# A two-layer transformer block with experts: the smallest expert class holds 32 tokens instead of 64

## The chip, the core and the metric

The kernel runs on one core of one Trainium2 chip. Its time is the time of one execution on the device in microseconds (us). A program is written once for each engine: PE (TensorE, the matrix engine; PEld is its loading of weights), DVE (VectorE), ACT (ScalarE) and SP (SyncE, which here only issues DMA transfers). Engines and transfers meet through semaphores.

## What is computed

Two layers over 256 tokens of width 1024. Each layer has a token mixer (four kinds of attention, four heads each) and a feed-forward part, both between an adaptive norm and a residual. The feed-forward part of layer 0 is dense. That of layer 1 is a mixture of eight experts, of which each token uses the two with the largest router logits:

```python
def _swiglu(h, wg, wu, wd):
    return (jax.nn.silu(h @ wg) * (h @ wu)) @ wd

logits = h.astype(jnp.float32) @ w_router.astype(jnp.float32)     # 8 experts
top_val, top_idx = lax.top_k(logits, TOP_K_EXPERTS)               # 2 of 8
gate = jax.nn.softmax(top_val, axis=-1)
...
return _swiglu(xb, w_gate[e], w_up[e], w_down[e])                 # 1024 -> 3584 -> 1024
...
y_assign = ys[dest] * g_s[:, None].astype(h.dtype)
return jnp.zeros_like(h).at[tok_s].add(y_assign)
```

All is float32. With the inputs of `setup_inputs()` the reference sends 25, 54, 96, 70, 145, 10, 84 and 28 tokens to experts 0 to 7.

## The kernel before

**Everything ahead of the experts** (layer 0 whole, layer 1 up to the router) is one straight program for each engine and is not touched by the change, but for the line numbers. It ends at 749 us of the profiled execution.

**The experts** run one after the other in a hardware loop over `r` (L967, eight rounds). Each expert's 3584 hidden channels are cut into four steps (`ES`), so there are 32 steps `J`. A step needs 896 gate columns, 896 up columns (1024 rows each) and 896 down rows (1024 columns). SP loads them with a program of its own (L521 to L538) in a fixed order: four pieces of gate weights, four of up weights (896 KB each), two pieces of down weights (1536 KB) and a last one in two halves (256 KB each), 10,752 KB or 11.01 MB a step. **The buffer holds one step.** A piece of step J+1 is issued only when PE has used the same piece of step J for the last time (`g_used`, `u_used`, `d_used`), and SP issues strictly in order.

**Classes.** DVE sorts each expert by its number of tokens against `CAPS` into class 1 to 4, and each engine branches on it (L971, L1371, L1565). The code of all four classes stands in the loop, one after the other. `UNITS` says how the tokens of a class are laid out on PE's columns: "half" is 64 tokens, so that two groups of 448 hidden channels are worked on side by side; "quarter" is 32 tokens, four groups side by side (gate low, gate high, up low, up high, all in bank 2); "wide" is 128 tokens and one group. Class 1 is one half, class 2 a half and a quarter, class 3 a wide and a quarter. By the counts above, experts 0, 1, 5 and 7 are class 1, experts 2, 3 and 6 class 2, expert 4 class 3, and class 4 isn't used.

**A step of class 1 on PE**: `hidden` for gate and for up (32 products, L829), each waiting for its own weight pieces as they land; ACT's SiLU and DVE's product with the up half (L1342); `turn_hidden` transposes the result (L854, L859); ACT copies it (L1522); `down` multiplies with the down rows (14 products, L879). Class 2 does the same, then `quarter` (L841, 32 products) between `hidden` and `turn_hidden`, and a second, smaller transposition and `down` (28 products) at the end. In class 2 and 3 the last user of gate and up weights is `quarter`, so `g_used` and `u_used` are signalled there.

**At the end of an expert** ACT (L1557) and DVE (L1350 to L1361) copy the outputs out of PSUM, PE scatters them to the tokens (`scatter`, L954 and L962), DVE adds them up (L1380), clears the banks, and the loop turns to the next expert. DVE makes the next expert's window of tokens (`window`, L1312) while PE is still in the last step.

Of the kernel before, what the change touches and what calls it, by code (L numbers as in the profile page):

```python
# [30 lines left out]
ACT = mybir.ActivationFunctionType  # L31
AX_X = mybir.AxisListType.X

P = 128
T = 256
D = 1024
KC = D // P
# [15 lines left out]
ES = 4  # L53
# [166 lines left out]
def ada_after(l, at):  # L220
# [3 lines left out]
    while i < len(STREAM) and STREAM[i][0] == "ada":  # L224
# [7 lines left out]

CAPS = (64, 96, 160)
UNITS = {1: [("half", 0)], 2: [("half", 0), ("quarter", 64)], 3: [("wide", 0), ("quarter", 128)],
         4: [("wide", 0), ("wide", 128)]}
ITEMS = {n: sum(2 if kind == "wide" else 1 for kind, _ in units) for n, units in UNITS.items()}

# [33 lines left out]
def build(nc, x, c, w_ada, b_ada, g_mix, w_in, g_heads, w_out, g_ffn, w_ff_gate, w_ff_up, w_ff_down,  # L273
          w_router, w_exp_gate, w_exp_up, w_exp_down, g_final, ctab_in, btab_in, out):
    with ExitStack() as ctx:
# [59 lines left out]
        ys = part(2 * D).rearrange("p (q n) -> p q n", q=2)  # L335
# [32 lines left out]
        hs = moe[:, 2 * EH:4 * EH].rearrange("p (b n) -> p b n", b=2)  # L368
# [7 lines left out]
        bank = [ctx.enter_context(nc.psum_tensor(f"bank{i}", [P, CW], F32)) for i in range(8)]  # L376
# [25 lines left out]
        full_u = [sem(f"up_in{i}") for i in range(KP)]  # L402
# [39 lines left out]
        def done(n, i):  # L442

            return i + 1 if i < ITEMS[n] - 1 else 4
# [104 lines left out]
        def _(pe):  # L549
# [284 lines left out]
                    elif (n == 1 and k == KC - 2) or (not last_item and k == KC - 1):  # L834
                        last.then_inc((eg_p, eu_p)[a], 3 if n == 1 else before_last(n, i))

            def quarter(t0, ks):

                for k in ks:
                    for q, w in enumerate((eg, eg, eu, eu)):  # L840
                        last = mm(bank[2][32 * q:32 * q + 32, 0:EH], xsT[:, k, t0:t0 + 32],  # L841
                                  w[:, k, (q % 2) * EH:(q % 2 + 1) * EH], start=(k == 0), stop=(k == KC - 1))
                        if k % 2 and q % 2:
                            last.then_inc(u_used if q == 3 else g_used, 1)

            def turn_hidden(J, n, i, kind, o, c=0):

                if kind != "quarter":
                    pe.wait_ge(eh_v, 4 * J + done(n, i))
                rows_ = slice(64, P) if kind == "quarter" else slice(0, P)  # L850
                h, one_ = hs[rows_, i % 2, :], ident[rows_, rows_]
                m = 64 if kind == "quarter" else P
                for t in range(3):
                    nc.tensor.transpose(o[:, t * m:(t + 1) * m], h[:, t * P:(t + 1) * P], one_)  # L854
                if kind == "wide":
                    last = mm(o[64 * c:64 * c + 64, 3 * P:4 * P], h[:, 3 * P:EH], ident, start=True, stop=True)
                else:
                    for c2 in range(2):
                        last = mm(o[64 * c2:64 * c2 + 64, 3 * m:3 * m + m // 2], h[:, 3 * P:EH],  # L859
                                  one_[:, c2 * m // 2:(c2 + 1) * m // 2], start=True, stop=True)  # L860
                last.then_inc(et_p, share(n, i))
# [25 lines left out]
            def step(r, J, n):  # L887
# [1 line left out]
                A = UNITS[n][0]  # L889
                B = UNITS[n][1] if len(UNITS[n]) > 1 else None  # L890
                if n == 1:
                    hidden(J, n, 0, 0, A)
                    hidden(J, n, 0, 1, A)
                    turn_hidden(J, n, 0, "half", bank[3])
                    pe.wait_ge(yzero_v, r + 1)
                    down(J, n, 0, ALL, (0,))
                elif n == 2:
                    hidden(J, n, 0, 0, A)
# [79 lines left out]
        def _(ve):  # L978
# [4 lines left out]
            def signal(ins, s):  # L983

                ins.then_inc(s, 1)
                count[s.name] = count.get(s.name, 0) + 1
# [358 lines left out]
            def expert_end(r, n):  # L1345

                window(r + 1)
                tiles = 2 if n > 2 else 1
                ve.wait_ge(sgt_p, r + 1)
                last = nc.vector.tensor_copy(selgT[:, 0:tiles, :].rearrange("p q n -> p (q n)"), bank[0][:, 0:tiles * T])  # L1350
                if n > 1:
                    ve.wait_ge(d_used, 3 * ES * r + 3 * ES)
                if n in (2, 3):
                    s0, q = (64, 0) if n == 2 else (0, 1)
                    for c in range(4):
                        last = nc.vector.tensor_copy(ys[s0:s0 + 32, q, c * T:(c + 1) * T],
                                                     bank[6][32 * c:32 * c + 32, 0:T])
                elif n == 4:
                    for hf in range(2):
                        last = nc.vector.tensor_copy(ys[:, 1, hf * CW:(hf + 1) * CW], bank[6 + hf][:, :])  # L1360
                last.then_inc(ys_v, 1)  # L1361
# [2 lines left out]
            clear_banks()  # L1364
            scatter_weights(0)
            signal(nc.vector.memset(ys, 0.0), dv)
            signal(nc.vector.memset(yacc, 0.0), yacc_v)
            with ve.Fori(0, NE) as r:
                which = class_of(ve, r)
# [28 lines left out]
        def _(ae):  # L1398
# [126 lines left out]
            def step(J, n):  # L1525

                if n == 1:
                    silu(J, n, 0)
                    turned_hidden(J, n, 0, 0, 0, bank[3])
                elif n == 2:  # L1530
                    silu(J, n, 0)
                    turned_hidden(J, n, 0, 0, 0, bank[3])
# [19 lines left out]
            def expert_end(r, n):  # L1552

                ae.wait_ge(d_used, 3 * ES * r + 3 * ES)
                for hf in range(2):
                    if UNITS[n][0][0] == "half":
                        ins = act(ys[0:64, 0, hf * CW:(hf + 1) * CW], bank[4][64 * hf:64 * hf + 64, :], ACT.Copy)  # L1557
                    else:
                        ins = act(ys[:, 0, hf * CW:(hf + 1) * CW], bank[4 + hf][:, :], ACT.Copy)
                ins.then_inc(ys_a, 1)  # L1560
# [26 lines left out]
```

## Time and profile before

| | us |
|---|---|
| median of 3 runs | 1781.99 |
| lowest, highest | 1771.41, 1783.42 |
| the profiled execution: its own time | 1774.51 |
| its span, from the first to the last instruction | 1772.7 |
| start of expert 0 to start of expert 1 | 749.6 to 850.6 |
| expert 1 | 850.6 to 973.1 |
| expert 2 | 973.1 to 1098.1 |
| expert 3 | 1098.1 to 1221.4 |
| expert 4 | 1221.4 to 1426.4 |
| last product of expert 7 ends | 1758.3 |

Each expert's start is the start of its first product on PE; expert 1's is taken as the end of the scatter before it, at 850.59, since PE stands idle behind that (the rows show it). PE is busy for 90% of the span, and DMA for 74% of it. The chain of waits follows the work that ended last back through the trace: each of its rows is a start time, a length and what was under way. A row "PE bank L830 x64" is 64 records, two for each of 32 products, since each float32 product appears as two matrix records and two weight loads.

### The profile page before, as it was taken

The page shows a single profiled execution, that of the slowest core. Times are in us where ns is not written, and L with a number is a line of the kernel's source. Part 1 is how long each engine was busy: PE and PEld are TensorE (multiplying, and loading weights), DVE is VectorE, ACT ScalarE, POOL GpSimd, SP SyncE. Part 2 cuts the span into 40 slices and gives each one's busy share as a digit, 9 for nine tenths or more (in the row PEclk, how much of TensorE's full clock was granted, in tenths as well). Part 3 has the DMA queues.
Part 4 walks back from the last instruction along what each step waited for, and adds up shares of the span by engine and source line. Part 5 has one row for each costly group of instructions (what it writes and reads, how often), then busy time and mean ns, then how long its engine had stood idle before and what let it go on. Part 6 is the DMA issues. An engine that isn't in the chain of part 4 may idle for free.

```text
span 1772.7 us, 19682 instructions
## 1 busy us (share of the span) xinstructions
PE 1594.6 (90%) x8282; PEld 872.2 (49%) x8283; DVE 409.1 (23%) x867; ACT 226.2 (13%) x439; POOL 0.2 (0%) x4
## 2 busy tenths in 40 slices
PE   5999889999989998797597999999999998999975
PEld 5778658777658784432132333334444433333321
DVE  4265523323333633400101002002000110100103
ACT  1122210000011321110011011111011001111101
POOL 0000000000000000000000000000000000000000
PEclk9999899999989998799799999999999999999998
DMA  9955525665745440099999999897666599999995
GB/s 348 326 203 177 190 95 190 237 237 190 262 136 181 167 181 19 3 378 371 342 389 371 382 378 370 327 389 279 248 248 235 208 327 388 370 389 371 389 371 217
DMA packets 168108, 482.18 MB, mean 272 GB/s; under 512 B 10472, under 2 KB 20992, under 8 KB 167936
## 3 DMA queue, kind: packets, MB, share of 16 engines
q1 hardware_dynamic: 168064, 481.57, 74.3%
q8 instruction: 30, 0.49, 0.1%
q14 instruction: 14, 0.11, 0.0%
HBM read 480.49 MB, written 1.05 MB: 272 GB/s over the span
## 4 chain that ended last, share of the span: by engine, by line
PE 74%; SPq 8%; DVE 8%; DMA 6%; issue 3%; ACT 2%; DVEq 0%; ACTq 0%
PE bank L830 14%; PE bank L879 10%; PE bank L640 7%; SPq L527 6%; PE bank L841 6%; PE bank L777 6%; PE bank L826 6%; PE bank L791 4%; DMA ring<-in_w_exp_down 4%; DVE acc L1004 4%; PE bank L759 3%; PE bank L873 3%; PE bank L634 2%; PE bank L962 2%; SPq L533 1%
## 5 line engine op out<-in xcount | busy, mean ns | idle before, releaser
L830 PE MATMUL bank<-ring,hT 128*64 128x448 f32 x1792 | 353.8, 545 | 45.6 <-issue 19.3
L879 PE MATMUL bank<-ring,bt 128*32 128x256 f32 (+1 forms) x1680 | 239.9, 495 | 24.5 <-DMA ring<-in_w_exp_down 12.3
L830 PEld LDWEIGHTS bank<-ring,hT 128*64 128x64 f32 x1792 | 130.0, 137 | 265.9 <-issue 205.9
L1342 DVE TENSOR_TENSOR bt<-bt,bank 128x448 f32<-128x448 f32 (+1 forms) x52 | 32.4, 622 | 807.6 <-PE bank L830 555.0
L879 PEld LDWEIGHTS bank<-ring,bt 128*32 128x32 f32 (+1 forms) x1680 | 86.0, 125 | 160.5 <-issue 119.1
L777 PE MATMUL bank<-hT,ring 128*128 128x256 f32 x704 | 156.0, 383 | 1.2 <-DVE hT L1075 1.2
L640 PE MATMUL bank<-hT,ring 128*128 128x256 f32 x640 | 152.9, 396 | 2.3 <-ACT hT L1424 1.2
L777 PEld LDWEIGHTS bank<-hT,ring 128*128 128x128 f32 x704 | 134.6, 192 | 21.7 <-issue 1.9
L640 PEld LDWEIGHTS bank<-hT,ring 128*128 128x128 f32 x640 | 124.4, 198 | 23.4 <-DVE hT L1075 3.1
L1004 DVE SCALAR_TENSOR_TENSOR acc<-ring,cond,acc 128x512 f32<-128x512 f32 x160 | 120.3, 752 | 5.6
L841 PE MATMUL bank<-ring,hT 128*32 128x448 f32 x1024 | 102.9, 542 | 0.0
L826 PE MATMUL bank<-ring,hT 128*128 128x448 f32 x256 | 98.2, 542 | 0.0
L791 PE MATMUL bank<-ring,arena 128*128 128x512 f32 x176 | 76.7, 594 | 0.0
L1510 ACT ACT_TABLE_LOAD x32 | 41.1, 1283 | 249.5 <-PE bank L830 246.6
L826 PEld LDWEIGHTS bank<-ring,hT 128*128 128x128 f32 x256 | 48.1, 190 | 47.0 <-issue 47.0
L1522 ACT ACTIVATE bt<-bank 128x448 f32<-128x448 f32 (+1 forms) x44 | 21.0, 476 | 331.1 <-PE bank L859 331.1
L759 PE MATMUL bank<-ring,hT 128*128 128x512 f32 x128 | 59.2, 625 | 2.0 <-DVE hT L1072 2.0
L634 PE MATMUL bank<-ring,hT 128*128 128x256 f32 x256 | 57.1, 381 | 3.1 <-ACT arena L1444 3.1
L841 PEld LDWEIGHTS bank<-ring,hT 128*32 128x32 f32 x1024 | 30.0, 109 | 59.8 <-issue 58.9
L634 PEld LDWEIGHTS bank<-ring,hT 128*128 128x128 f32 x256 | 48.1, 190 | 10.8 <-issue 4.5
L791 PEld LDWEIGHTS bank<-ring,arena 128*128 128x128 f32 x176 | 33.1, 190 | 39.7 <-issue 39.7
L873 PE MATMUL bank<-ring,bt 128*128 128x512 f32 x112 | 50.2, 600 | 0.0
(204 smaller groups left out, 999.8 us busy)
## 6 DMA issues: line engine op xcount, KB each, us to landing
ring<-in_w_exp_gate SPq DMA_DIRECT2D x128, 896.0 KB, 10.4
ring<-in_w_exp_up SPq DMA_DIRECT2D x128, 896.0 KB, 15.1
ring<-in_w_exp_down SPq DMA_DIRECT2D x64, 1536.0 KB, 16.3
ring<-in_w_ada SPq DMA_DIRECT2D x24, 2048.0 KB, 10.4
ring<-in_w_in SPq DMA_DIRECT2D x10, 2048.0 KB, 11.1
ring<-in_w_exp_down SPq DMA_DIRECT2D x64, 256.0 KB, 16.8
ring<-in_w_ff_gate SPq DMA_DIRECT2D x5, 2048.0 KB, 18.6
ring<-in_w_ff_up SPq DMA_DIRECT2D x5, 2048.0 KB, 14.0
```

The costliest lines, as they stand in the source:

```text
L527: sp.dma_start(dst[:, 2 * i:2 * i + 2, :], w[0, e, 2 * i * P:2 * (i + 1) * P, j0:j0 + EW].rearrange("(c p) n -> p c n", p=P))\
L634: last = mm(o[:, b * T:(b + 1) * T], hT[:, k, b * P:(b + 1) * P], w[:, k, :], start=(k == 0), stop=(k == KC - 1))
L640: last = mm(o[:, 0:T], w[:, k, t * P:(t + 1) * P], hT[:, k, :], start=(k == 0), stop=(k == KC - 1))
L759: last = mm(bank[4 + 2 * hf + b][:, :], hT[:, k, b * P:(b + 1) * P], w[:, k, :], start=(k == 0), stop=(k == KC - 1))
L777: last = mm(bank[n % 2][:, a * T:(a + 1) * T], w[a][:, k, t * P:(t + 1) * P], hT[:, k, :], start=(k == 0), stop=(k == KC - 1))
L791: last = mm(bank[4 + 2 * hf + b][:, :], ffT[:, (j - 1) % 2, r, b * P:(b + 1) * P], w[:, r, hf * CW:(hf + 1) * CW], start=(j == 1 and r == ...
L826: last = mm(o[:, 0:EH], xsT[:, k, t0:t0 + P], w[:, k, c * EH:(c + 1) * EH], start=(k == 0), stop=(k == KC - 1))
L830: last = mm(o[64 * c2:64 * c2 + 64, 0:EH], xsT[:, k, t0:t0 + 64], w[:, k, c2 * EH:(c2 + 1) * EH], start=(k == 0), stop=(k == KC - 1))
L841: last = mm(bank[2][32 * q:32 * q + 32, 0:EH], xsT[:, k, t0:t0 + 32], w[:, k, (q % 2) * EH:(q % 2 + 1) * EH], start=(k == 0), stop=(k == K ...
L873: last = mm(bank[4 + 2 * u + hf][:, :], hsT[:, u, t * P:(t + 1) * P], ed[:, t, hf * CW:(hf + 1) * CW], start=False, stop=True, skip_group_ ...
L879: last = mm(bank[4 + 2 * u][m * c:m * c + m, 0:D // parts], hsT[:, u, at_:at_ + m], ed[:, t, c * (D // parts):(c + 1) * (D // parts)], sta ...
L1004: ins = stt(acc[:, :], w[:, k, :], cond[:, k:k + 1], acc[:, :], ALU.mult, ALU.add)
```

## The change

`CAPS` starts at 32, and class 1 is one unit "quarter" instead of one "half". An expert with 33 to 64 tokens is now class 2. With the counts above experts 0, 5 and 7 stay in class 1, which has a new body, and expert 1 (54 tokens) moves to class 2; the others keep both class and body.

In class 1 PE now works gate and up side by side, `k` by `k`, and waits for a gate piece and the up piece with the same number together. It signals `g_used` and `u_used` from the same loop. `down` has 28 products of 256 columns instead of 14 of 512. The transposition handles half as many columns, except for one transposition of the full height. The output copies cover 32 instead of 64 tokens and are shared by ACT and DVE; DVE waits for `d_used` there. DVE clears `hs` once, ahead of the loop.

```diff
--- before.py
+++ after.py
@@ -232,8 +232,8 @@
 
 
 
-CAPS = (64, 96, 160)
-UNITS = {1: [("half", 0)], 2: [("half", 0), ("quarter", 64)], 3: [("wide", 0), ("quarter", 128)],
+CAPS = (32, 96, 160)
+UNITS = {1: [("quarter", 0)], 2: [("half", 0), ("quarter", 64)], 3: [("wide", 0), ("quarter", 128)],
          4: [("wide", 0), ("wide", 128)]}
 ITEMS = {n: sum(2 if kind == "wide" else 1 for kind, _ in units) for n, units in UNITS.items()}
 
@@ -834,23 +834,32 @@
                     elif (n == 1 and k == KC - 2) or (not last_item and k == KC - 1):
                         last.then_inc((eg_p, eu_p)[a], 3 if n == 1 else before_last(n, i))
 
-            def quarter(t0, ks):
+            def quarter(t0, ks, J=None):
 
                 for k in ks:
+                    if J is not None and k % 2 == 0:
+                        pe.wait_ge(full_g[k // 2], 16 * J + 16)
+                        pe.wait_ge(full_u[k // 2], 16 * J + 16)
                     for q, w in enumerate((eg, eg, eu, eu)):
                         last = mm(bank[2][32 * q:32 * q + 32, 0:EH], xsT[:, k, t0:t0 + 32],
                                   w[:, k, (q % 2) * EH:(q % 2 + 1) * EH], start=(k == 0), stop=(k == KC - 1))
                         if k % 2 and q % 2:
                             last.then_inc(u_used if q == 3 else g_used, 1)
+                        elif J is not None and k == KC - 1:
+                            last.then_inc(eu_p if q == 2 else eg_p, 3)
 
             def turn_hidden(J, n, i, kind, o, c=0):
 
                 if kind != "quarter":
                     pe.wait_ge(eh_v, 4 * J + done(n, i))
+                if n == 1:
+                    pe.wait_ge(eh_v, 4 * J + done(n, i))
+                    nc.tensor.transpose(o[:, 0:P], hs[:, 0, 0:P], ident)
+                    o = o[:, 64:]
                 rows_ = slice(64, P) if kind == "quarter" else slice(0, P)
                 h, one_ = hs[rows_, i % 2, :], ident[rows_, rows_]
                 m = 64 if kind == "quarter" else P
-                for t in range(3):
+                for t in range(1 if n == 1 else 0, 3):
                     nc.tensor.transpose(o[:, t * m:(t + 1) * m], h[:, t * P:(t + 1) * P], one_)
                 if kind == "wide":
                     last = mm(o[64 * c:64 * c + 64, 3 * P:4 * P], h[:, 3 * P:EH], ident, start=True, stop=True)
@@ -889,10 +898,9 @@
                 A = UNITS[n][0]
                 B = UNITS[n][1] if len(UNITS[n]) > 1 else None
                 if n == 1:
-                    hidden(J, n, 0, 0, A)
-                    hidden(J, n, 0, 1, A)
-                    turn_hidden(J, n, 0, "half", bank[3])
+                    quarter(A[1], range(KC), J)
                     pe.wait_ge(yzero_v, r + 1)
+                    turn_hidden(J, n, 0, "quarter", bank[3])
                     down(J, n, 0, ALL, (0,))
                 elif n == 2:
                     hidden(J, n, 0, 0, A)
@@ -1348,13 +1356,13 @@
                 tiles = 2 if n > 2 else 1
                 ve.wait_ge(sgt_p, r + 1)
                 last = nc.vector.tensor_copy(selgT[:, 0:tiles, :].rearrange("p q n -> p (q n)"), bank[0][:, 0:tiles * T])
-                if n > 1:
-                    ve.wait_ge(d_used, 3 * ES * r + 3 * ES)
-                if n in (2, 3):
-                    s0, q = (64, 0) if n == 2 else (0, 1)
-                    for c in range(4):
+                ve.wait_ge(d_used, 3 * ES * r + 3 * ES)
+                if n < 4:
+                    s0, q = ((0, 0), (64, 0), (0, 1))[n - 1]
+                    o = bank[4 if n == 1 else 6]
+                    for c in ((2, 3) if n == 1 else range(4)):
                         last = nc.vector.tensor_copy(ys[s0:s0 + 32, q, c * T:(c + 1) * T],
-                                                     bank[6][32 * c:32 * c + 32, 0:T])
+                                                     o[32 * c:32 * c + 32, 0:T])
                 elif n == 4:
                     for hf in range(2):
                         last = nc.vector.tensor_copy(ys[:, 1, hf * CW:(hf + 1) * CW], bank[6 + hf][:, :])
@@ -1364,6 +1372,8 @@
             clear_banks()
             scatter_weights(0)
             signal(nc.vector.memset(ys, 0.0), dv)
+            signal(nc.vector.memset(hs, 0.0), dv)
+            own(dv)
             signal(nc.vector.memset(yacc, 0.0), yacc_v)
             with ve.Fori(0, NE) as r:
                 which = class_of(ve, r)
@@ -1526,7 +1536,7 @@
 
                 if n == 1:
                     silu(J, n, 0)
-                    turned_hidden(J, n, 0, 0, 0, bank[3])
+                    turned_hidden(J, n, 0, 0, 0, bank[3][:, 64:])
                 elif n == 2:
                     silu(J, n, 0)
                     turned_hidden(J, n, 0, 0, 0, bank[3])
@@ -1553,7 +1563,9 @@
 
                 ae.wait_ge(d_used, 3 * ES * r + 3 * ES)
                 for hf in range(2):
-                    if UNITS[n][0][0] == "half":
+                    if n == 1:
+                        ins = act(ys[0:32, 0, hf * T:(hf + 1) * T], bank[4][32 * hf:32 * hf + 32, 0:T], ACT.Copy)
+                    elif n == 2:
                         ins = act(ys[0:64, 0, hf * CW:(hf + 1) * CW], bank[4][64 * hf:64 * hf + 64, :], ACT.Copy)
                     else:
                         ins = act(ys[:, 0, hf * CW:(hf + 1) * CW], bank[4 + hf][:, :], ACT.Copy)
```

How the order moves. The first place is class 1 on PE, inside the loop over experts (`ring` holds the weights, `hT` the expert's tokens, `bt` the hidden values, `arena` the outputs and scatter matrices). Before:

```order
L972 ISA
L830 MATMUL bank<-ring,hT 64x448 x32
L849 ISA
L854 MATMUL bank<-ct,bt 128x128 x3
L859 MATMUL bank<-ct,bt 64x64 x2
L879 MATMUL bank<-ring,bt 64x512 x12
L870 ISA
L879 MATMUL bank<-ring,bt 64x512 x2
L972 REGISTER_ALU
L972 COMPARE_AND_BRANCH
```

Of the change:

```order
L844 MATMUL bank<-ring,hT 32x448 x32
L856 ISA
L857 MATMUL bank<-ct,bt 128x128
L863 MATMUL bank<-ct,bt 128x64 x2
L868 MATMUL bank<-ct,bt 64x32 x2
L888 MATMUL bank<-ring,bt 32x256 x24
L879 ISA
L888 MATMUL bank<-ring,bt 32x256 x4
```

The first phase has as many products as before, each for 32 instead of 64 tokens; the down phase has twice as many, each of half the width. The class-1 code on PE is longer by 14 products.

The second place is class 1 on DVE with the end of the expert (the row `bt<-bt,bank` is the product of SiLU and up half, `hT<-ring` the next expert's window, `arena<-bank` the copies out of PSUM). Before:

```order
L1342 TENSOR_TENSOR bt<-bt,bank 128x448
L1372 REGISTER_ALU
L1372 COMPARE_AND_BRANCH
L1311 ISA
L1311 TENSOR_LOAD route_i
L1311 ISA x2
L1312 ISA
L1312 COPY hT<-ring 128x2048
L1350 COPY arena<-bank 128x256
```

Of the change:

```order
L1350 TENSOR_TENSOR bt<-bt,bank 64x448
L1382 REGISTER_ALU
L1382 COMPARE_AND_BRANCH
L1319 ISA
L1319 TENSOR_LOAD route_i
L1319 ISA x2
L1320 ISA
L1320 COPY hT<-ring 128x2048
L1358 COPY arena<-bank 128x256
L1359 ISA
L1364 COPY arena<-bank 32x256 x2
```

Two small copies and a wait have come behind the copy of the scatter matrix; the rest stands as it did.

## Rows read from the trace of the kernel before

**Rows 1.** The page: chain that ended last, shares by engine

```profile
PE 74%; SPq 8%; DVE 8%; DMA 6%; issue 3%; ACT 2%; DVEq 0%; ACTq 0%
```

**Rows 2.** Chain of waits, experts 0 and 1: start us, length us, what

```profile
749.62 12.27 PE bank L830 x64
...
764.24 6.23 PE bank L879 x28
...
841.86 3.70 PE bank L879 x16
846.92 3.67 PE bank L962 x8
850.59 19.28 issue
869.87 14.62 PE bank L830 x64
...
962.72 5.38 PE bank L879 x16
...
973.13 12.18 PE bank L830 x64
```

**Rows 3.** Chain of waits, class 2: experts 2 and 3, start of 4

```profile
985.31 4.65 PE bank L841 x48
...
1002.37 12.18 PE bank L830 x64
...
1085.06 5.03 PE bank L879 x64
...
1098.11 12.18 PE bank L830 x64
...
1210.04 5.03 PE bank L879 x64
...
1221.39 18.04 PE bank L826 x48
```

**Rows 4.** Chain of waits, experts 5 to 7

```profile
1426.38 12.20 PE bank L830 x64
...
1537.10 1.72 PE bank L830 x8
...
1749.58 3.68 PE bank L879 x16
```

**Rows 5.** Stretches: length, busy PE, PEld, DVE, ACT, POOL, clock, DMA share, GB/s

```profile
850.60:869.90 19.30, 0.03 (x2) 0.03 (x2) 3.13 (x7) 0.00 (x0) 0.00 (x0) 0.59 1.01 367
869.90:874.00 4.10, 4.10 (x12) 1.48 (x14) 0.00 (x0) 0.00 (x0) 0.00 (x0) 0.50 0.34 121
...
1432.00:1752.00 320.00, 286.15 (x1684) 104.96 (x1682) 26.57 (x45) 34.41 (x48) 0.00 (x0) 0.97 1.03 377
```

**Rows 6.** Timeline of SP's DMA issues: start us, length us, line, target, count

```profile
751.38 4.88 SPq L527 DMA_DIRECT2D ring<-in_w_exp_gate  x4
...
873.16 5.70 SPq L527 DMA_DIRECT2D ring<-in_w_exp_gate  x4
...
1111.96 5.76 SPq L527 DMA_DIRECT2D ring<-in_w_exp_gate  x4
```

**Rows 7.** DMA queue q8, packets, MB, share: whole span, 0:733, 848:872

```profile
q8 instruction: 30, 0.49, 0.1%
...
q8 instruction: 24, 0.39, 0.2%
...
q8 instruction: 6, 0.10, 2.6%
```

**Rows 8.** Groups by line and shape, experts only: busy us, mean ns | idle before

```profile
L830 PE MATMUL bank<-ring,hT 128*64 128x448 f32 x1792 | 353.8, 545 | 45.6 <-issue 19.3 <-DMA ring<-in_w_exp_up 12.7 <-DMA ring<-in_w_exp_gate 10.8
...
L841 PE MATMUL bank<-ring,hT 128*32 128x448 f32 x1024 | 102.9, 542 | 0.0
...
L879 PE MATMUL bank<-ring,bt 128*32 128x256 f32 x896 | 51.7, 381 | 0.0
```

## The prediction

> **What bounds the kernel now.** I read the chain of waits first. By shares it is a PE kernel [rows 1], but the share is a mean over stages, so I followed the chain through the experts in order of time, and then asked in each stage whether PE or the weight stream is late.
>
> *Class 1 is late on DMA.* Expert 0 starts at 749.62 with its first step's weights in place: 12.27 us of hidden products, then 6.23 us of down products [rows 2]. A step of pure PE work, with what lies between, is thus under 21 us. The last down weights of its fourth step let PE go on only at 841.86 [rows 2], 92 us after the start. The stream moves 377 GB/s when nothing stops it [rows 5]; 11.01 MB a step at that rate are 29.2 us. Three steps of it from the first issue at 751.38 [rows 6] end at 839, which is where PE waits.
>
> *Class 2 is late on PE, by a hair.* A step of class 2 lasts from 973.13 to 1002.37, 29.24 us, all of it PE, with `quarter` starting at 985.31 [rows 2, 3]. To an undisturbed stream this is the same as 29.2. The difference between the classes is not in the step, but in **when the first weight piece is given back**. In class 1 that is 751.38, 1.8 us after the expert's start [rows 2, 6]. In class 2 gate piece 0 is free only in `quarter`: expert 3 starts at 1098.11, and the stream restarts at 1111.96, 13.85 us later [rows 3, 6].
>
> *The PE gap at 850.59.* Behind expert 0's scatter PE waits 19.28 us for nothing that a semaphore shows [rows 2], and its clock falls to 0.59 [rows 5]. The weights of expert 1's first step stream in meanwhile at 367 GB/s, and by 869.9 they are nearly done: in the next 4.1 us the DMA share is 0.34 [rows 5]. The next step's issue follows at 873.16 [rows 6], so the stream stands for only some 2 us. What PE waits for is its own code: of 30 packets on the instruction queue q8, 24 come ahead of 733 us, six in 848 to 872, and so none later [rows 7]. The first round skips the code of classes 2 to 4 and jumps back; that code is fetched through the full DMA queues, six packets in about three round trips of 6.4 us. It happens once.
>
> **The Trainium skill on this wait.** "Runtime: NRT & Kernel Launch", section "Instruction fetch mechanics", says that an engine's code is streamed in 16 KiB blocks, that a jump out of what is held waits for a fetch, and that PE holds 128 KiB, 2048 instructions. The six packets of 0.10 MB agree with the block size. By my count of the built program the loop over experts is some 1,710 PE instructions before and 1,770 after, so by the page's figure it still fits and this wait stays a single one; what would follow if it didn't is a rival below.
>
> **The change, part by part.** Weights, SP's order and the work of experts 2, 3, 4 and 6 are the same.
>
> *Class 1's hidden products get cheaper where it isn't wanted.* A record of `quarter` costs 102.9/1024 = 100 ns against 353.8/1792 = 197 ns for `hidden` [rows 8]: 64 records are 6.4 instead of 12.3 us. Down: 56 records at 51.7/896 = 58 ns are 3.2 instead of 6.2 us [rows 2, 8]. That is 9 us less PE in each of 12 steps, 108 us in sum, all of it under the stream, which takes 29.2 us a step whatever PE does. The new wait pairs gate piece 0 with up piece 0, which lands four pieces (9.4 us of stream) later, and what queues behind it on PE is only the other products; by then six pieces, 7.2 MB or 19 us of stream, are still issued, so the release is not late and SP does not run dry. At the start of an expert both pieces are there and piece 0 is free after 16 records of 100 ns, 1.6 us, as now. The stream of expert 0 and of experts 5 to 7 therefore keeps its times. For 5 to 7 the check is that eleven steps (121 MB at 377 GB/s, 321 us) from 1428 (expert 5's start at 1426.38 plus 1.6) end at 1749, and PE's last weights came at 1749.58 [rows 4]. Sum of this part: 0. The later SiLU (it now needs all of the gate, behind the last piece) is covered too: down weights land 9 us behind the last up piece. Without that cover it would cost under 2 us.
>
> *Tails.* What is left behind the last weights gets shorter at experts 0 and 7: one down tile (0.9 to 0.45 us) and smaller output copies. I take -0.8 us each. Against it stands the clock: PE now idles in one piece while four gate pieces and the first up piece land (4.6 MB, 12 us of each step), and after the idle stretch at 850.59 the first 64 records took 14.62 instead of 12.2 us [rows 2, 3]; the last down products may run as at 962.72, 5.38 instead of 3.70 us for the same 16 records [rows 2]. With a slow scatter this is up to +3.5 us. I take -0.8 for expert 0 and 0 for expert 7.
>
> *Expert 1 moves to class 2.* This is the term that decides. It starts where PE comes out of the gap: 850.59 - 0.8 + 19.3 = 869.1. The code of class 1 is 56 PE instructions longer (14 products, four instructions each), which shifts what lies in which block: between nothing and one more round trip of 6.4 us, of which the last would be short, as the weights are in by then. I take +2: 871.1. Its hidden products run cold for 14.6 us, `quarter` starts at 885.7 and gives piece 0 back 1.7 us later, at 887.4. The stream has run dry at about 872. **It now stands for 15 us instead of 2.** From there PE sets the pace: 2.5 us of cold start, four steps of 29.24 us, and the expert's end. From the start of the last 64 down records to the next expert it took 13.05 us at 1085.06 and 11.35 at 1210.04 [rows 3], so 8.0 and 6.3 behind the records; I take 7.2. Expert 1 ends at 871.1 + 2.5 + 117.0 + 7.2 = 997.8 instead of 973.1: **+24.7 us**. Nothing gives this back: expert 2 before started with a full stream too and took 125.0 us, PE-bound; as a successor of class 2 it should take what expert 3 took, 123.3 to 125.0: -0.8. Experts 3 and 4 are PE-bound and move whole. Experts 5 to 7 are a chain of stream hung on expert 5's start, so they move whole too.
>
> *DVE's clearing of `hs`* ahead of the loop (under 1.8 us) lies beside the first hidden products: 0.
>
> Sum: 24.7 - 0.8 = **+23.9 us**, the rest 0. On the profiled execution, 1774.5, that is 1798.4; its time is 7.5 under the median, and on the median the sum would give 1805.9. I forecast **1800 us**, nearer the profiled one, since the sum was made on it.
>
> **Rivals.**
>
> *The stream does not break (not slower).* If PE's code is there sooner, expert 1 starts sooner. The new piece 0 has to be free before 872, so the start has to lie before 872 - 12.2 - 1.7 = 858, that is the gap has to be shorter than about 8 us instead of 19.3. For it: the longer class 1 reaches further into its neighbour's code, which could be fetched in the quiet of the first steps. Against: three of the four classes' blocks are still ahead of the jump. Then hidden products wait for the stream, expert 1 ends at about 977, and the time is +4 us: 1779 to 1786.
>
> *The loop's code no longer stays in.* If the 56 instructions push it over what PE holds, the gap of 850.59 comes at every change of expert. At four PE-bound changes that is 4 times 19.3 us on top, +77, and some of it at the others: 1875 to 1900. For it: the loop grew by a few per cent, and the trace shows only that the old size fits. By the page's figure it fits still.
>
> *The clock.* If class 1 idles enough for half clock all through, its step is 2 times 9.6 us and some 4 of waits, 23 us, still under 29.2; only the tails grow. +27 to +30 us: 1801 to 1812.
>
> *Faster.* Experts 0, 5 and 7 have 108 us less PE work; this would only show if the stream were not what they wait for, against rows 4 and 5.
>
> **How the numbers follow.** Forecast as worked out (+17 to +27) 0.61, stream unbroken 0.15, code pushed out 0.08, clock low in class 1 0.12, faster or other 0.04. The range leaves out the pushed-out code and the lower half of the unbroken stream: 1785 to 1813. A measurement tells about 1% from no change (17.8 us). The forecast is 1.3%, so about a tenth of its chance falls under that with the unbroken stream: same 0.22; slower 0.75; faster 0.03.
>
> **What would show it.** In the changed kernel: an idle stretch of PE behind expert 0 of 19 to 26 us with six or seven packets on q8; the next gate issue 15 to 18 us behind expert 1's first product; a DMA share near 0 between; steps of 29.2 us in expert 1, and expert 2 starting near 998; experts 5 to 7 as long as before, 332 us from 5's start to 7's last product. I am wrong if q8 moves after the first round, if the gate issue comes early, or if class 1's steps shorten.

## The result

The changed kernel takes 1799.18 us, the median of 4 runs (1792.11 to 1802.74), against 1776.70 us for the kernel before (4 runs of the same session, 1769.66 to 1783.42). The ratio is **1.0138 (95% interval 1.0088 to 1.0188)**: 22.5 us slower, where the forecast was 1800 us and a sum of +23.9 us. Run twice more later, each time beside before, it came out at 1.0168 (1.0118 to 1.0218; I had expected 1.010 to 1.015 of that run) and 1.0112 (1.0070 to 1.0154).

The execution profiled took 1802.74 us, its span 1800.8 us. Its chain of waits, in the stretches that rows 2 show of before (start us, length us, what; L844 is `quarter`, L888 `down`, L970 `scatter`):

```profile
751.64 6.23 PE bank L844 x62
...
845.07 3.17 PE bank L888 x32
...
850.25 3.70 PE bank L970 x8
853.95 17.82 issue
871.77 14.59 PE bank L830 x64
...
903.42 12.18 PE bank L830 x64
...
997.46 12.18 PE bank L830 x64
...
1120.74 12.18 PE bank L830 x64
...
1245.72 18.04 PE bank L826 x48
...
1450.95 6.19 PE bank L844 x62
...
1562.39 1.72 PE bank L830 x8
...
1775.37 3.64 PE bank L888 x32
...
1781.01 5.42 PE bank L970 x8
```

Expert 0 starts 2.0 us later than before (nothing ahead of it was changed) and takes 102.3 us where before took 101.0 [rows 2]. The gap behind it is 17.8 instead of 19.3 us. Then expert 1, now class 2, takes 125.7 us to expert 2's start, where before took 103.3. Experts 2 and 3 take 123.3 and 125.0 us (before 125.0 and 123.3 [rows 3]), expert 4 205.2 (205.0), and experts 5 to 7 up to the end of the last scatter 335.5 (331.9).

SP's timeline, for rows 6:

```profile
753.37 4.88 SPq L527 DMA_DIRECT2D ring<-in_w_exp_gate  x4
...
888.03 5.76 SPq L527 DMA_DIRECT2D ring<-in_w_exp_gate  x4
```

and the stretches of expert 0, the gap, the break in the stream, the rest of expert 1, and experts 5 to 7 (length, then busy PE, PEld, DVE, ACT and POOL, granted clock, DMA share, GB/s):

```profile
753.00:850.00 97.00, 55.26 (x498) 19.96 (x490) 9.86 (x14) 9.45 (x14) 0.00 (x0) 0.75 1.01 364
853.00:871.00 18.00, 0.95 (x3) 0.12 (x1) 3.82 (x8) 0.00 (x0) 0.00 (x0) 0.58 1.03 389
...
874.00:888.00 14.00, 14.00 (x80) 5.10 (x80) 0.62 (x1) 0.54 (x1) 0.00 (x0) 0.91 0.04 13
888.00:997.00 109.00, 106.75 (x834) 40.02 (x826) 9.43 (x16) 13.70 (x21) 0.00 (x0) 1.00 1.01 371
1460.00:1775.00 315.00, 231.35 (x1844) 85.10 (x1843) 26.80 (x46) 30.59 (x46) 0.00 (x0) 0.84 1.03 380
```

In class 1 PE is busy for 55 of 97 us and the stream goes on at 364 GB/s; in the last row PE has 55 us less work than rows 5 show for a stretch of about the same length, and the stream is as full as before (1.03). After expert 1's start the stream stands for 14 us (share 0.04), until `quarter` gives the first piece back 16.3 us after the start. The groups of the experts say the same by line (busy us, mean ns, idle before):

```profile
L844 PE MATMUL bank<-ring,hT 128*32 128x448 f32 x2048 | 221.1, 576 | 77.2 <-DMA ring<-in_w_exp_up 74.4
...
L830 PE MATMUL bank<-ring,hT 128*64 128x448 f32 x1024 | 198.7, 546 | 18.9 <-issue 17.8
```

What PE no longer works in class 1 it waits for up pieces instead: 74.4 us ahead of L844.

### The profile page after: what moved, and what is told of

Same layout as the page of the kernel before. It is cut to its first block, busy times and chain, and to the rows that moved or that the text cites. A ratio compares the mean times of both kernels' runs of the same rounds, so it can differ in the third digit from the quotient of the medians.

```text
span 1800.8 us, 21465 instructions
## 1 busy us (share of the span) xinstructions
PE 1559.8 (87%) x9126; PEld 862.0 (48%) x9127; DVE 416.6 (23%) x882; ACT 226.1 (13%) x447; POOL 0.2 (0%) x4
## 4 chain that ended last, share of the span: by engine, by line
PE 74%; DMA 11%; DVE 7%; SPq 4%; issue 2%; ACT 1%; DVEq 0%
PE bank L830 10%; PE bank L844 10%; PE bank L888 9%; DMA ring<-in_w_exp_up 8%; PE bank L640 7%; PE bank L777 6%; PE bank L826 5%; PE bank L791 4%; DVE acc L1012 4%; PE bank L759 3%; SPq L527 3%; PE bank L882 3%; DMA ring<-in_w_exp_down 2%; PE bank L634 2%; PE bank L970 2%
## 5 line engine op out<-in xcount | busy, mean ns | idle before, releaser
L844 PE MATMUL bank<-ring,hT 128*32 128x448 f32 x2048 | 221.1, 576 | 77.2 <-DMA ring<-in_w_exp_up 74.4
L888 PE MATMUL bank<-ring,bt 128*32 128x256 f32 (+1 forms) x2240 | 232.6, 477 | 15.8 <-DMA ring<-in_w_exp_down 9.6
L1350 DVE TENSOR_TENSOR bt<-bt,bank 64x448 f32<-64x448 f32 (+1 forms) x56 | 34.9, 623 | 834.9 <-ACT bt L1518 388.5
L830 PE MATMUL bank<-ring,hT 128*64 128x448 f32 x1024 | 198.7, 546 | 18.9 <-issue 17.8
L844 PEld LDWEIGHTS bank<-ring,hT 128*32 128x32 f32 x2048 | 66.0, 115 | 214.0 <-issue 212.7
L888 PEld LDWEIGHTS bank<-ring,bt 128*32 128x32 f32 (+1 forms) x2240 | 89.5, 127 | 144.5 <-issue 93.4
L830 PEld LDWEIGHTS bank<-ring,hT 128*64 128x64 f32 x1024 | 72.6, 138 | 140.7 <-issue 136.9
L640 PEld LDWEIGHTS bank<-hT,ring 128*128 128x128 f32 x640 | 126.1, 201 | 23.9 <-DVE hT L1083 3.1
L1532 ACT ACTIVATE bt<-bank 128x224 f32<-128x224 f32 (+1 forms) x48 | 20.1, 420 | 304.6 <-PE bank L868 304.6
L970 PE MATMUL bank<-arena 128*128 128x512 f32 x72 | 39.8, 707 | 15.6 <-DVE arena L1364 15.6
L634 PEld LDWEIGHTS bank<-ring,hT 128*128 128x128 f32 x256 | 48.1, 190 | 10.8 <-issue 4.5
```

The source lines that it names most:

```text
L634: last = mm(o[:, b * T:(b + 1) * T], hT[:, k, b * P:(b + 1) * P], w[:, k, :], start=(k == 0), stop=(k == KC - 1))
L640: last = mm(o[:, 0:T], w[:, k, t * P:(t + 1) * P], hT[:, k, :], start=(k == 0), stop=(k == KC - 1))
L830: last = mm(o[64 * c2:64 * c2 + 64, 0:EH], xsT[:, k, t0:t0 + 64], w[:, k, c2 * EH:(c2 + 1) * EH], start=(k == 0), stop=(k == KC - 1))
L888: last = mm(bank[4 + 2 * u][m * c:m * c + m, 0:D // parts], hsT[:, u, at_:at_ + m], ed[:, t, c * (D // parts):(c + 1) * (D // parts)], sta ...
L970: last = mm(bank[4 + 2 * b + hf][:, :], selgT[:, q, b * P:(b + 1) * P], ys[:, q, hf * CW:(hf + 1) * CW], start=(q == 0), stop=(q == tiles[ ...
```

## The experiments

Theory: expert 1's move to class 2 is the whole loss. In class 1 PE has 8 us a step to spare against the stream and makes up for the gap behind expert 0; in class 2 it has none, so the gap and 29.2 us a step add up. Rivals: the new class-1 body costs something itself; the break in the stream, not PE's pace, makes expert 1 long; the gap is something else than code.

The kernels' stages, read off their traces as above (us; "0" and the rest are experts up to the start of the next one's first product or, for 0 and 7, to the end of the scatter; one execution each; each ratio is to before in its own session, where before's median was 1775.6 to 1776.7):

| kernel | median, ratio to before | 0 | gap | 1 | 2 to 4 | 5 to 7 |
|---|---|---|---|---|---|---|
| before | 1776.7 | 101.0 | 19.3 | 103.3 | 453.3 | 331.9 |
| changed | 1799.2, 1.0138 | 102.3 | 17.8 | 125.7 | 453.5 | 335.5 |
| changed, second | 1804.0, 1.0168 | 103.0 | 18.0 | 125.3 | 453.5 | 331.0 |
| changed, third | 1797.5, 1.0112 | 105.6 | 14.9 | 125.7 | 453.5 | 335.1 |
| cap 32, old body | 1799.3, 1.0129 | 98.6 | 19.5 | 125.1 | 453.5 | 339.0 |
| quarter and half | 1780.8, 1.0022 | 105.1 | 15.6 | 102.2 | 456.2 | 338.8 |
| changed, no class-4 code | 1803.1, 1.0154 | 101.3 | 12.2 | 125.6 | 453.5 | 339.0 |
| the same, again | 1801.6, 1.0108 | 103.6 | 12.0 | 126.3 | 451.7 | 344.8 |
| changed, class-1 code last | 1780.0, 1.0031 | 102.2 | none | 128.8 | 453.5 | 332.5 |
| before, class-1 code last | 1779.3, 1.0012 | 102.4 | none | 119.7 | 455.0 | 335.2 |
| changed, fewer down rows | 1768.6, 0.9988 | 93.3 | 18.3 | 126.5 | 451.8 | 312.5 |
| five classes, no class-4 code | 1781.2, 1.0020 | 103.2 | 18.4 | 98.9 | 452.6 | 338.5 |

The column "5 to 7" follows the weight stream. With all weights loaded it runs from 331.0 to 344.8 us, the changed kernel alone from 331.0 to 335.5. The four executions without class-4 code on PE ("quarter and half" is one of them) are all at 338.5 or more, and six of the seven with it at 335.5 or less; "cap 32, old body", at 339.0, breaks the pattern. No run looks for a cause, so this column can hide a few us of any edit.

The gap and expert 0 have to be read together. In the changed kernel's three traces PE's first product of expert 1 starts 17.9, 18.0 and 17.9 us after the first code packet behind expert 0 (packets at 853.9, 851.4 and 848.5 us). In the third the gap is only 14.9 us because the scatter before it ran at the lower clock, most of its records in 1.06 instead of 0.59 us, while the fetch was already under way:

```profile
844.94 6.55 PE bank L970 x8
851.49 14.91 issue
```

So its 3 us more in expert 0 are 3 us less in the gap. The same holds for "quarter and half".

**The class without the body.** The kernel before, with one line changed:

```diff
-CAPS = (64, 96, 160)
+CAPS = (32, 96, 160)
```

> The kernel before with CAPS (32, 96, 160) and nothing else: experts 0, 5 and 7 keep the old half body, expert 1 is class 2. Theory (the loss is expert 1's move, the cheaper body of class 1 lies under the weight stream): as slow as the changed kernel or 1 to 4 us less, since its tails are not cold, so 20 us above before, ratio about 1.011; expert 1 takes about 143 us with the gap, expert 5 to the end as before. Rival 1 (the lighter body is worth something): clearly slower than the changed kernel, up to 108 us. Rival 2 (the new body costs, by its paired waits or by the clock): within 5 us of before.

Chain of waits of this kernel behind expert 0:

```profile
845.00 19.51 issue
864.51 13.99 PE bank L830 x64
...
989.61 12.18 PE bank L830 x64
```

Measured: 1799.29 us, ratio 1.0129 (1.0094 to 1.0164). It is the changed kernel's time, with PE's old 20 us of work a step in class 1. Expert 1 takes 125.1 us behind the gap. So the cheaper body is worth nothing in time, in either direction that these runs can tell, and the whole loss comes with expert 1's class.

**The body without the class.** The changed kernel with the old half body for 33 to 64 tokens, in the place of class 4:

```diff
-         4: [("wide", 0), ("wide", 128)]}
+         4: [("half", 0)]}
...
+                elif n == 4:
+                    hidden(J, n, 0, 0, A)
+                    hidden(J, n, 0, 1, A)
+                    turn_hidden(J, n, 0, "half", bank[3])
+                    pe.wait_ge(yzero_v, r + 1)
+                    down(J, n, 0, ALL, (0,))
...
-            then(ts(total, sums, float(CAPS[0]), 1.0, ALU.is_gt, ALU.add))
-            for cap in CAPS[1:]:
+            then(ts(total, sums, float(CAPS[0]), -1.0, ALU.is_gt, ALU.add))
+            for _ in range(2):
+                then(stt(total, sums, float(CAPS[0]), total, ALU.is_gt, ALU.add))
+                then(stt(total, sums, 64.0, total, ALU.is_le, ALU.add))
+            for cap in CAPS[1:2]:
```

> The changed kernel with one more class: up to 32 tokens the new quarter body, 33 to 64 the old half body, which stands in the place of the unused class of 160 to 256 tokens. Expert 1 is on the half body again. Theory: all of the loss goes but the longer tails of experts 0 and 7: 0 to 4 us above before. Rival 2 (the new body costs by itself): 10 us or more above before. If the cheap body were a gain, it would be under before.

Measured: 1780.80 us, ratio 1.0022 (0.9996 to 1.0048). Expert 1 is back at 102.2 us behind the gap. Both halves of the change are now priced: the class some 23 us (by the run before, 17 to 29), the body 4 us (its interval is -0.7 to +8.5). So the body is worth nothing within some us; closer than that these runs don't tell.

**A shorter jump.** Class 4's code, which no expert of these inputs runs, is left out of PE's loop:

```diff
-                for n in range(1, 5):
+                for n in range(1, 4):
                     with pe.If(which == n):
```

> The changed kernel without the code of the unused fourth class on TensorE (467 instructions less to jump over; no expert of these inputs is in it). Theory (PE waits behind expert 0 for its own code, and expert 1 in class 2 can't catch up): four packets behind expert 0 on the instruction queue instead of five, the gap 11 to 13 us instead of 17.8, and the time 5 to 7 us under the changed kernel. Rival (the gap is a wait for weights or semaphores): gap and time unchanged.

Chain of waits of this kernel behind expert 0, and its instruction queue in 845 to 866 us; then the queue of the changed kernel in 853 to 874 us:

```profile
847.73 3.70 PE bank L970 x8
851.43 12.23 issue
...
q8 instruction: 4, 0.07, 1.8%
```

```profile
q8 instruction: 5, 0.08, 2.1%
```

One packet and 5.6 us less: the gap behaves as a wait for code. But the time, 1803.05 us, ratio 1.0154 (1.0118 to 1.0190), is not lower, against my expectation. In the trace the saving reaches expert 5's start (692.6 us after expert 0's, against 699.3), and half of it is gone by the last scatter, 3.2 us less than in the changed kernel's first trace. So I ran it again beside the changed kernel.

> The changed kernel without the fourth class's code on TensorE, a second time, now in one call with the changed kernel itself, since the first time its trace showed the gap 5.6 us and expert 1 as much shorter and the total did not. Theory: gap 12 us, expert 1 137 to 138 us, median 3 to 7 us under the changed kernel of this call. Rival (the 6 us are given back in the stages that follow the stream): experts 5 to 7 together 5 us longer than in the changed kernel, in this execution too, and the medians equal.

> The changed kernel, the yardstick of this call. Theory: 1.3 to 1.7% above before; gap 17 to 20 us, experts 2 to 4 within 2 us of the earlier traces, expert 5's start to the last product of expert 7 between 331 and 339 us, as in the executions seen so far.

Measured: 1801.59 us, ratio 1.0108 (1.0068 to 1.0148), and 1797.45 us, 1.0112 (1.0070 to 1.0154) for the changed kernel. The gaps are 12.0 and 14.9 us (12.1 and 17.9 from the first code packet). The changed kernel is under the 1.3% and its gap under the 17 us that I had expected of it; the gap is explained above. The totals are equal within what six runs tell. Up to expert 5's start the kernel without class-4 code is again 6 us shorter (693.6 against 699.7), and again its stream stage is longer (344.8 against 335.1), as the rival said. Whether that is the scatter of single executions or a way in which the gain is given back, these runs do not settle.

**No jump under load.** Class 1's code is placed last on PE, so that expert 0 already has to get past the others, when the DMA queues are idle; the wait for the expert's tokens goes into the step:

```diff
+                pe.wait_ge(xsT_v, r + 1)
                 A = UNITS[n][0]
...
-                pe.wait_ge(xsT_v, r + 1)
-                for n in range(1, 5):
+                for n in (2, 3, 4, 1):
                     with pe.If(which == n):
```

> The changed kernel with the code of class 1 placed last in TensorE's loop (classes 2, 3, 4, 1), so that expert 0 already has to jump over the others, while the DMA queues are idle. Theory: the code packets come around 747 to 758 us, the gap of 17.8 us behind expert 0 goes, expert 0 starts 3 to 8 us later; the next gate issue after expert 0 comes near or before the end of the stream; the time is 8 to 15 us under the changed kernel, but still 5 to 12 above before. Rival (the gap belongs to the turn of the loop, not to the fetched code): gap and time stay.

Chain of waits of this kernel, SP's timeline behind expert 0, and the instruction queue in 735 to 752 us (in 760 to 1775 us it has no packet):

```profile
744.24 2.86 issue
747.11 7.93 PE bank L844 x62
...
861.00 1.72 PE bank L830 x8
...
890.89 1.72 PE bank L830 x8
...
951.22 1.73 PE bank L830 x8
...
977.96 12.17 PE bank L830 x63
```

```profile
864.39 5.76 SPq L527 DMA_DIRECT2D ring<-in_w_exp_gate  x4
```

```profile
q8 instruction: 6, 0.10, 2.7%
```

Measured: 1780.02 us, ratio 1.0031 (1.0003 to 1.0059), 17 to 24 us under the changed kernel's three medians, more than the 8 to 15 expected. The later start of expert 0 that I had expected isn't there: the first packet comes at 736.3 us, while PE is still in its last product ahead of the experts, which ends at 742.1. From that packet to the first product it takes 10.8 us, of which only 2.9 are a wait of their own; behind expert 0 it takes 17.9, nearly all of it waiting. Expert 1, still class 2, now ends every hidden phase on the arrival of an up piece (the short L830 rows at 861.0, 890.9 and 951.2): PE has caught up with the stream. This is the rival "the stream does not break", made true; I had priced it at 977 us for expert 1's end, and it ended at 977.96.

**The gap alone.** The same edit on the kernel before.

> The kernel before with TensorE's code of class 1 placed last in the loop, as in the earlier experiment on the changed kernel. Theory (with expert 1 in class 1 the gap is made up for by PE's spare 8 us a step, and only the 2 us for which the stream stood are to be had, against 3 us of later start): within 5 us of before, no gap behind expert 0. Rival (the gap costs before its full 19 us too): 10 to 15 us under before.

Measured: 1779.30 us, ratio 1.0012 (0.9981 to 1.0043). Its chain of waits:

```profile
744.49 3.03 issue
747.51 13.90 PE bank L830 x64
...
969.49 12.18 PE bank L830 x64
```

The whole 19.3 us gap is gone from the chain and the time is the same, since expert 1 in class 1 then waits for the stream: 119.7 us, where gap and body took 122.5. A wait that the next stage can catch up on is worth nothing.

The four kernels together, from expert 0's start to expert 5's: class 1 with the gap (before) 676.8 us, without it 677.0; class 2 with the gap (changed) 699.3, without it 684.3. So the gap alone costs nothing, class 2 alone 7 to 8 us, and both together 22.5: two thirds of the loss is there only when both are. These are single executions; by the ratios it is +2 us, +6 and +20 to +30.

**A lighter stream.** The changed kernel loads two of three row tiles of each large down piece; the products over the third run on what the buffer held:

```diff
-                    sp.dma_start(ed[:, 3 * i:3 * i + 3, :],
-                                 w_exp_down[0, e, r0:r0 + 3 * P, :].rearrange("(c p) n -> p c n", p=P)).then_inc(full_d[i], 16)
+                    sp.dma_start(ed[:, 3 * i:3 * i + 2, :],
+                                 w_exp_down[0, e, r0:r0 + 2 * P, :].rearrange("(c p) n -> p c n", p=P)).then_inc(full_d[i], 16)
```

> The changed kernel with a third of the down rows of each large down piece not loaded (two tiles of three; the products over the third run on what the buffer held before), so a step streams 9.96 instead of 11.01 MB, and all of PE's work is left. Theory (class 1 follows the stream, class 2 and 3 follow PE): expert 0 about 8 us shorter, expert 1 behind the gap (about 126 us) and experts 2, 3 and 4 unchanged, expert 5 about 8 to 11 us shorter, expert 7 8 to 15 us shorter: 25 to 35 us under the changed kernel. Rival (expert 1 is long since its stream starts late): expert 1 behind the gap is 8 us shorter too. Rival (class 1 is bound by something on PE): its stages keep their length.

Its chain of waits around expert 1, and its stretch from 888 to 980 us:

```profile
838.83 3.70 PE bank L970 x8
842.53 18.33 issue
...
981.92 5.40 PE bank L970 x8
```

```profile
888.00:980.00 92.00, 91.66 (x738) 34.61 (x736) 5.26 (x8) 9.47 (x17) 0.00 (x0) 1.00 0.94 345
```

Measured: 1768.59 us, 29 to 35 us under the changed kernel's medians. Expert 0 is 9 us shorter or more and experts 5 to 7 are 18 to 23 us shorter, of which 6 to 7 in expert 5, where I had expected 8 to 11. **Expert 1 keeps its length (126.5 us)**, with PE busy for 91.7 of 92 us. The break in the stream is still there (a share of 0.01 from 861 to 876 us, where the next piece is issued); but each step now has 2.8 us less to stream behind it, and expert 1 gains nothing by that. So it is not the late stream that makes expert 1 long.

**More code.** The old half body as a fifth class, so that nothing is dropped. By my count of the compiled program PE's loop has 1998 instructions, against 1706 before and 1766 of the changed kernel.

```diff
-         4: [("wide", 0), ("wide", 128)]}
+         4: [("wide", 0), ("wide", 128)], 5: [("half", 0)]}
...
-                for n in range(1, 5):
+                for n in range(1, 6):
```

> The changed kernel with the old half body as a fifth class behind the fourth (33 to 64 tokens), so that all old classes stay. TensorE's loop has 1998 instructions instead of 1766. Theory (the loop's code is fetched once, as long as it stays under the 2048 instructions that the Trainium skill's page Runtime: NRT & Kernel Launch gives): one or two more packets on the instruction queue behind expert 0 and none later, time 1779 to 1787. Rival (code is pushed out of what TensorE holds): packets and a gap of 10 to 25 us at every change of expert, 60 to 110 us above before.

The page's row for its instruction queue, and its chain of waits at each change of expert:

```profile
q8 instruction: 92, 1.51, 0.4%
```

```profile
853.79 35.92 issue
...
990.33 8.90 issue
...
1125.83 18.78 issue
...
1270.20 25.21 issue
...
1502.76 7.22 issue
...
1615.50 28.97 issue
...
1771.01 17.48 issue
```

Measured: 1910.14 us, ratio 1.0751 (1.0681 to 1.0821), 134 us above before. There are 92 packets instead of 30 and a gap at each of the seven changes of expert, 142 us in all. My theory was wrong here: I took the figure of the Trainium skill, "Runtime: NRT & Kernel Launch", section "Instruction fetch mechanics" (2048 instructions for PE), as the bound. By the trace 1998 already do not stay in, and the measurement decides. Why the bound lies lower, no run shows. So I left class 4 out of PE's loop of this same kernel:

```diff
-                for n in range(1, 6):
+                for n in (1, 2, 3, 5):
```

> The kernel with five classes, of which TensorE's loop leaves out the code of the unused fourth: 1531 instead of 1998 instructions, all else as in the five-class kernel. Theory (its 134 us were code that no longer stays in): packets only ahead of expert 0 and behind it, none later, 1776 to 1784 us, as with the four classes quarter, half, 96 and 160. Rival (the fifth class costs by its numbering, or by what the other engines do): within 20 us of 1910.

Measured: 1781.21 us, ratio 1.0020 (0.9982 to 1.0057), no packet behind 880 us. The 129 us between the two are the code on PE and nothing else of the fifth class.

## Why the prediction was right

**Expert 1 decides: right, and within 5 us in two of three traces.** The sum had the gap and expert 1 at 21.3 + 126.7 = 148.0 us instead of 122.5, 25.5 longer (the 24.7 of the text has expert 0's -0.8 in it). It was 143.5, 21.0 longer (143.3 and 140.6 in the other two traces). Behind the gap I had worked out 126.7 us (cold start, four steps of 29.24, the end) and 125.7 came. The gap is the mis-sized term: I took 19.3 + 2, and it was 17.8, 18.0 and 14.9. With it two of the signs failed: a stretch of 19 to 26 us, and six or seven packets. The longer class 1 does shift the blocks, but in the helpful direction: one packet now comes at 766 us (763 and 760 in the other two traces), in the first steps, so five instead of six are left behind expert 0. The kernel with cap 32 and the old body has no such packet and keeps six and 19.5 us. That was the argument "for" in the rival of the unbroken stream, and it held in part.

**That 1800 met 1799.18 so closely is in part luck.** The sum stood on a choice between 1774.5 and 1782.0. In the profiled pair the span grew by 28.1 us: 2.0 ahead of the experts, 1.3 in expert 0, 21.0 in the gap and expert 1, 0.2 in experts 2 to 4 and 3.5 in 5 to 7. The sum had 25.5 for the gap and expert 1, -0.8 each for experts 0 and 2, and nothing for the rest. What it had too high and what it left out nearly made up for each other, and all but the 21.0 is of a size that executions of one kernel differ by.

**The cause I set in bold was half of it.** "It now stands for 15 us instead of 2" was right as an observation (14 us at a share of 0.04, next issue 16.3 us after the start, 16.3 forecast). But the sum was never made from it, and the lighter stream shows that it does not matter: expert 1 takes 125.7 us with 11.01 MB a step and 126.5 with 9.96. PE's pace does it. The break is its mark, since a class whose first piece comes back late leaves the stream idle as soon as PE is behind.

**The cheap body is worth nothing: right**, by the old body at the same time, and by the stream's share of 1.01 to 1.03. One step of that argument is miscounted: the six pieces behind the first up piece are 6.4 MB or 17 us of stream, not 7.2 and 19; the release came in time all the same. And PE saved less than the 9 us a step worked out: 55 us in the eight steps of experts 5 and 7, at a mean clock of 0.84 instead of 0.97.

**Tails: the sign was wrong at expert 0, and open at expert 7.** I took -0.8 us and 0. From the last wait for down weights to the end of the scatter expert 0 took 8.9, 9.1 and 9.6 us in the three traces, against 8.7 before [rows 2], and expert 7 11.1, 9.4 and 7.5, against 8.7 before [rows 4 and the end of scatter at 1758.3]. The 5.42 us of the last scatter at 1781.01 are in the first trace alone; in the others it took 3.71 and 3.72. So the lower clock can cost the tail some 2 us, and not in every execution. What else expert 0 took beyond before (1.3 to 4.6 us in all) lies ahead of its last down weights, in the stream, or is paid back in the gap as shown above.

**Experts 5 to 7 keep their times: right within what one trace tells**, 331.0 to 335.5 against 331.9, though a single execution moves more than the effects looked for.

**The rivals.** Code pushed out of PE had 8 in 100 and a price of +100 to +125 us in all. It did not happen at 1766 instructions, and happens at 1998 with +134. The unbroken stream was a true alternative: moving code by hand brings it about. The low clock came in part: in class 1 the granted clock fell to 0.75 in expert 0 and, over experts 5 to 7, to 0.84, not to 0.5 all through, and its price of 3 to 6 us on top of the sum can't be told in the medians, which are 21 to 28 us above before. Faster was right to have little: 55 us less work on PE in the last stretch brought no time.

## What to carry to other kernels

Price a stage by what it can catch up on, not by its own length. Class 1 and class 2 both take 29 us a step, yet class 1 absorbed a 19 us stall whole and class 2 passed on 15 of 17.8 us. So a step that is level with its stream is already too long behind a stall. And with code that branches in a hardware loop, count the instructions of the loop and look at when the instruction queue moves: the order in which the bodies stand decided 17 to 24 us of the changed kernel here, and one body more cost 129.

## What the runs showed of the hardware

- TensorE jumping over code that it doesn't hold yet waits for it. From the first code packet to the first product it took 19.5 us before (six packets) and 17.9 to 18.0 in the changed kernel (five), with the weight stream at 367 to 389 GB/s, and 10.8 us for six packets with no weights moving (class-1 code last; in each case the last packet comes when PE is already at work). Fewer instructions to jump over shortened it to 12.3 and 12.1 us. In both kernels with class-1 code last only some 3 us are a wait of their own, since the fetch began beside PE's last product ahead of the experts. Of the 15 us between 17.8 and 2.9, then, about half comes from the idle queues and half from that overlap. That code and weights queue for the same DMA engines is argued from 10.8 against 17.9, not shown.
- A loop of 1766 instructions is fetched once (30 packets in all, the last at 873.5 us); one of 1998 is fetched in part at every change of expert, also from one expert of class 2 to the next, 7 to 36 us a time.
- The granted clock in expert 0 (class 1) fell to a mean of 0.75 (0.77 and 0.78 in the other two traces), with PE busy for 57% of the time in pieces; before, the like stretch had

```profile
751.00:841.00 90.00, 75.49 (x374) 28.32 (x370) 8.05 (x10) 9.48 (x12) 0.00 (x0) 0.98 1.01 367
```

  so less work on PE came with a lower clock for what was left: a record of `quarter` took 542 ns before, in classes 2 and 3 alone [rows 8], and 576 ns in the mean of all three classes in the changed kernel. It was free here but at the tails, since the stream set the pace.
- No version that loads all weights beats the kernel before: the best, class-1 code last on before and the five-class kernel without class 4, are at 1.0012 (0.9981 to 1.0043) and 1.0020 (0.9982 to 1.0057), so they can't be told from it.
